# Levels of the block inverses: one group of eight steps in place of two groups of four

## The reference

```python
a_mat = eye + jnp.where(pos[:, None] > pos[None, :], beta[..., :, None] * decay * kk, 0.0)
gamma = jnp.exp(G)
rhs = jnp.concatenate([beta[..., None] * v, (beta * gamma)[..., None] * k], axis=-1)
sol = lax.linalg.triangular_solve(a_mat, rhs, left_side=True, lower=True, unit_diagonal=True)
v_t, w = sol[..., :dv], sol[..., dv:]
...
def step(h, xc):
    qg_c, pqk_c, vt_c, w_c, kd_c, gl_c = xc
    u = vt_c - jnp.einsum('bhck,bhkv->bhcv', w_c, h)
    o = jnp.einsum('bhck,bhkv->bhcv', qg_c, h) + jnp.einsum('bhcm,bhmv->bhcv', pqk_c, u)
    h = h * gl_c[..., None, None] + jnp.einsum('bhck,bhcv->bhkv', kd_c, u)
    return h, o
```

## Time and profile before

| | us |
|---|---|
| median of 3 runs | 3616.95 (3615.12 to 3622.28) |
| the profiled execution | 3621.84 |
| its span, first to last instruction | 3619.7 |
| PE busy | 3285.3 (91%) |
| DVE busy | 1534.0 (42%) |
| ACT busy | 1114.4 (31%) |
| mean granted TensorE clock | 0.941 of 2.4 GHz |

### The profile page before, as it was taken

One profiled execution on the slowest core, in us unless ns is written; L12 is line 12 of the kernel. 1 busy time (PEld: TensorE's weight loads), 2 busy tenths in 40 slices (PEclk: granted clock), 3 DMA queues, 4 the chain that ended last, 5 costly groups with the idle time before them and its releaser, 6 DMA issues. The chain is left out here.

```text
span 3619.7 us, 55834 instructions
## 1 busy us (share of the span) xinstructions
PE 3285.3 (91%) x23074; PEld 2753.0 (76%) x23074; DVE 1534.0 (42%) x2177; ACT 1114.4 (31%) x1426; POOL 71.3 (2%) x64
## 2 busy tenths in 40 slices
PE   4699999999999999999599967777778899999997
PEld 0477777777777888887388956666667899999997
DVE  0432313323233234233622456666634655555554
ACT  2221222212222222222522434333324544444443
POOL 0000000000000000000000001101100000000000
PEclk8799999999999999999799978888879899999998
DMA  9464464654645322233033600000033455555552
GB/s 374 174 234 169 179 243 163 229 188 170 241 169 209 105 93 93 93 104 128 24 93 118 184 15 2 2 2 2 2 118 127 140 185 183 177 184 184 180 181 82
DMA packets 313074, 501.24 MB, mean 138 GB/s; under 512 B 7932, under 2 KB 248068, under 8 KB 293124
## 3 DMA queue, kind: packets, MB, share of 16 engines
q1 hardware_dynamic: 311552, 495.15, 40.1%
q0 software_dynamic: 576, 4.19, 0.3%
q10 hardware_dynamic: 836, 0.33, 0.0%
HBM read 497.55 MB, written 2.10 MB: 138 GB/s over the span
## 5 line engine op out<-in xcount | busy, mean ns | idle before, releaser
L1555 PE MATMUL ps<-xn,parts 128*128 128x256 f32 (+1 forms) x11184 | 1908.9, 332 | 75.1 <-DVE xn L1266 50.6
L1555 PEld LDWEIGHTS ps<-xn,parts 128*128 128x128 f32 x11184 | 1687.1, 191 | 315.9 <-issue 92.9
L1132 DVE TENSOR_TENSOR parts<-raw,parts 128x1024 fp32r<-128x1024 f32 x642 | 766.0, 1223 | 1188.1 <-ACT parts L639 1180.4
L639 ACT ACTIVATE parts<-raw 128x1024 fp32r<-128x1024 f32 x638 | 660.7, 1055 | 1416.7 <-PE ps L1555 876.5
L1555 PE MATMUL ps<-h_parts,parts 128*128 128x512 f32 (+1 forms) x4224 | 739.1, 337 | 0.0
L1555 PEld LDWEIGHTS ps<-h_parts,parts 128*128 128x128 f32 x4224 | 649.6, 190 | 87.9 <-DVE h_f L1148 5.9
L1164 DVE TENSOR_TENSOR acc<-acc,ps 128x512 f32<-128x512 f32 (+1 forms) x352 | 193.0, 554 | 302.9 <-PE ps L1555 302.8
L1555 PE MATMUL ps<-raw,cpad 128*32 128x512 f32 x1152 | 157.4, 661 | 28.5 <-DMA raw<-in_w_mod 26.2
L1555 PEld LDWEIGHTS ps<-raw,cpad 128*32 128x32 f32 x1152 | 30.1, 114 | 121.9 <-DMA raw<-in_w_mod 61.6
L649 ACT ACTIVATE h_parts<-h_f 128x1024 fp32r<-128x1024 f32 (+1 forms) x44 | 37.2, 845 | 258.1 <-DVE h_f L1148 258.1
L1311 PE MATMUL ps<-g_T,g_C 64*64 64x64 f32 x1280 | 60.4, 246 | 56.8 <-DVE g_T L948 43.0
(11 more groups left out here) (195 smaller groups left out, 1506.0 us busy)
## 6 DMA issues: line engine op xcount, KB each, us to landing
raw<-in_w_mod SPq DMA_DIRECT2D x144, 1024.0 KB, 7.8
raw<-in_w_gate SPq DMA_DIRECT2D x88, 1024.0 KB, 5.1
raw<-in_w_up SPq DMA_DIRECT2D x88, 1024.0 KB, 5.1
raw<-in_w_down SPq DMA_DIRECT2D x88, 1024.0 KB, 5.1
raw<-in_w_in SPq DMA_DIRECT2D x41, 1024.0 KB, 5.3
raw<-in_w_out SPq DMA_DIRECT2D x16, 1024.0 KB, 5.5
x_in<-in_ctx SPq DMA_DIRECT2D x2, 1024.0 KB, 6.7
x_in<-in_x SPq DMA_DIRECT2D x2, 1024.0 KB, 12.0
```

The lines of the kernel that those rows point to most:

```text
L639: nc.scalar.activation(parts[:, unit % PART_SLOTS, 0, :], raw[:, slot, b * UNIT:(b + 1) * UNIT], ACT.Copy).then_inc(hi_ready, 1)
L1132: nc.vector.tensor_tensor(parts[:, pslot, 1, :], raw[:, slot, b * UNIT:(b + 1) * UNIT], parts[:, pslot, 0, :].bitcast(F32), ALU.subtract)\
L1555: return nc.tensor.matmul(o, lhsT, rhs, start=start, stop=stop)
```

## The change

The two groups become one of eight chunks. `y_level`, `x_level`, `y_out` and `level` lose their argument g and are called where g is 0; the places of group 1 stay empty. PSUM banks 0, 2 and 4 are used with all their 512 columns, and banks 1, 3 and 5 no more by these parts. The counts of the semaphores are halved, and the arithmetic is the same.

```diff
-            def y_out(a, lv, g):
+            def y_out(a, lv):
-                a.wait("y_mm", 2 * lv + g + 1)
+                a.wait("y_mm", lv + 1)
                 if lv:
-                    a.wait("x_mm", 2 * (lv - 1) + g + 1)
-                nc.scalar.activation(flat(grp(g_Y, g)), pair_cols(0, g), ACT.Copy).then_inc(hs["y_ok"], 1)
+                    a.wait("x_mm", lv)
+                nc.scalar.activation(flat(g_Y[:]), ps[:, 0, :], ACT.Copy).then_inc(hs["y_ok"], 1)
...
-            def level(a, lv, g):
+            def level(a, lv):
                 if lv < 4:
-                    a.wait("xt_mm", 2 * lv + g + 1)
-                    a.wait("t_ok", solved(lv, g))
-                    nc.vector.tensor_tensor(flat(grp(g_T, g)), flat(grp(g_T, g)), pair_cols(2, g),
-                                            ALU.subtract).then_inc(hs["t_ok"], 1)
-                a.wait("x_mm", 2 * lv + g + 1)
-                a.wait("s_ok", solved(lv, g))
-                nc.vector.tensor_tensor(flat(grp(g_S, g)), flat(grp(g_S, g)), pair_cols(4, g),
-                                        ALU.subtract).then_inc(hs["s_ok"], 1)
+                    a.wait("xt_mm", lv + 1)
+                    a.wait("t_ok", solved(lv))
+                    nc.vector.tensor_tensor(flat(g_T[:]), flat(g_T[:]), ps[:, 2, :], ALU.subtract)\
+                        .then_inc(hs["t_ok"], 1)
+                a.wait("x_mm", lv + 1)
+                a.wait("s_ok", solved(lv))
+                nc.vector.tensor_tensor(flat(g_S[:]), flat(g_S[:]), ps[:, 4, :], ALU.subtract)\
+                    .then_inc(hs["s_ok"], 1)
...
-                        if a:
-                            level(a, lv, g)
+                        if a and g == 0:
+                            level(a, lv)
...
-            def y_level(a, lv, g):
-                a.wait("t_ok", solved(lv, g))
+            def y_level(a, lv):
+                a.wait("t_ok", solved(lv))
...
-                for s in range(4 * g, 4 * g + 4):
-                    last = pair_mm(g, CHUNK * (s % 4), g_C[:, lv, s, :], g_T[:, s, :])
+                for s in range(STEPS):
+                    last = pair_mm(0, CHUNK * s, g_C[:, lv, s, :], g_T[:, s, :])
                 inc(last, "y_mm")
...
-            def x_level(a, lv, g):
-                a.wait("y_ok", 2 * lv + g + 1)
-                a.wait("s_ok", solved(lv, g))
+            def x_level(a, lv):
+                a.wait("y_ok", lv + 1)
+                a.wait("s_ok", solved(lv))
...
                 if lv < 4:
-                    for s in range(4 * g, 4 * g + 4):
-                        last = pair_mm(2 + g, CHUNK * (s % 4), g_S[:, s, :], g_Y[:, s, :])
+                    for s in range(STEPS):
+                        last = pair_mm(2, CHUNK * s, g_S[:, s, :], g_Y[:, s, :])
                     inc(last, "xt_mm")
-                for s in range(4 * g, 4 * g + 4):
-                    last = pair_mm(4 + g, CHUNK * (s % 4), g_Y[:, s, :], g_S[:, s, :])
+                for s in range(STEPS):
+                    last = pair_mm(4, CHUNK * s, g_Y[:, s, :], g_S[:, s, :])
                 inc(last, "x_mm")
...
                     for g in range(2):
-                        if a:
-                            y_level(a, lv, g)
+                        if a and g == 0:
+                            y_level(a, lv)
```

More of the change, by code:

```diff
@@ L257, in every, with solved @@
             return m.unsqueeze(1).to_broadcast([P, STEPS, m.shape[1]])
[L259 to L265, removed]
+        def solved(lv):
+            return lv + 1
         ps = es.enter_context(nc.psum_tensor("ps", [P, 8, 512], F32))
@@ L308, in build_layer @@
             "vb_ok": 2, "e_mm": 2, "e_exp": 2, "kk_mm": 1, "qk_mm": 1, "n_half": 1, "n_ok": 1, "p_half": 1,
-            "p_ok": 1, "nT_mm": 1, "nT_ok": 1, "ts_half": 2, "t_ok": 9, "s_ok": 11, "c_mask": 5, "y_mm": 10,
-            "y_ok": 10, "xt_mm": 8, "x_mm": 10, "w_mm": 1, "vt_mm": 2, "w_ok": 2, "vt_ok": 2,
+            "p_ok": 1, "nT_mm": 1, "nT_ok": 1, "ts_half": 2, "t_ok": 5, "s_ok": 6, "c_mask": 5, "y_mm": 5,
+            "y_ok": 5, "xt_mm": 4, "x_mm": 5, "w_mm": 1, "vt_mm": 2, "w_ok": 2, "vt_ok": 2,
             "f_stage": 1, "f_a": 1, "f_mid_ok": 1, "f_b": 1, "f_v": 1, "f_hi": 1, "f_lo": 1,
@@ L595, in step @@
                     for g in range(2):
-                        if a:
-                            y_out(a, lv, g)
+                        if a and g == 0:
+                            y_out(a, lv)
                         if b and lv < 2:
@@ L1402, in transposed @@
                 inc(last, "nT_mm")
-            def y_level(a, lv, g):
-                a.wait("t_ok", solved(lv, g))
+            def y_level(a, lv):
+                a.wait("t_ok", solved(lv))
                 a.wait("c_mask", lv + 1)
                 if lv:
-                    a.wait("y_ok", 2 * (lv - 1) + g + 1)
+                    a.wait("y_ok", lv)
                 else:
@@ L1411, in y_level @@
                     a.wait("f_v")
-                for s in range(4 * g, 4 * g + 4):
-                    last = pair_mm(g, CHUNK * (s % 4), g_C[:, lv, s, :], g_T[:, s, :])
+                for s in range(STEPS):
+                    last = pair_mm(0, CHUNK * s, g_C[:, lv, s, :], g_T[:, s, :])
                 inc(last, "y_mm")
-            def x_level(a, lv, g):
-                a.wait("y_ok", 2 * lv + g + 1)
-                a.wait("s_ok", solved(lv, g))
+            def x_level(a, lv):
+                a.wait("y_ok", lv + 1)
+                a.wait("s_ok", solved(lv))
                 if lv == 0:
-                    a.wait("vb_ok", g + 1)
+                    a.wait("vb_ok")
                     a.wait("p_half")
                 if lv < 4:
-                    for s in range(4 * g, 4 * g + 4):
-                        last = pair_mm(2 + g, CHUNK * (s % 4), g_S[:, s, :], g_Y[:, s, :])
+                    for s in range(STEPS):
+                        last = pair_mm(2, CHUNK * s, g_S[:, s, :], g_Y[:, s, :])
                     inc(last, "xt_mm")
-                for s in range(4 * g, 4 * g + 4):
-                    last = pair_mm(4 + g, CHUNK * (s % 4), g_Y[:, s, :], g_S[:, s, :])
+                for s in range(STEPS):
+                    last = pair_mm(4, CHUNK * s, g_Y[:, s, :], g_S[:, s, :])
                 inc(last, "x_mm")
@@ L1539, in step @@
                             written_u(b, STEPS - 1)
-                        if a:
-                            x_level(a, lv, g)
+                        if a and g == 0:
+                            x_level(a, lv)
                         if b and lv < 2:
```

## The result

Over 20 runs each, the kernel before takes 3617.93 us (3615.04 to 3622.41) and the changed one 3625.59 us (3623.83 to 3630.35): 7.7 us more, ratio 1.002, interval [1.0013, 1.0027]. That lies in the range of the prediction (3611 to 3634), 4.6 us above its forecast and just over the 0.2% that it takes for the limit of a measurement: slower, to which it gave a chance of 0.26, against 0.66 for no difference that can be told.

The account below looks back on a forecast made before the run. The mixer was taken as a relay with no engine full, bound by late hand-overs. Terms 1.4 + 1.8 + 0.9 = +4.1 us took the profiled 3621.84 to 3625.9; with the median 4.9 lower, the forecast was 3621.0, range 3611 to 3634.

Parts of the forecast that it names:

- The prices of the instructions: Mixer: one 512-column DVE subtraction takes 0.684 us, one 512-column ACT copy 0.597 us, both taken from similar instructions.
- B: Rival, faster: DVE's time decides and hand-overs cost nothing; 2.8 us saved over nine levels, 3614 us; chance 0.11.
- The hand-overs in heads 1 to 6: Middle heads: wider copies and subtractions hand over later, +0.3 us a head (ends +0.1 and +0.6), +1.8 for six.
- Head 0: First head, no scan beside it: later hand-overs in levels 1 to 4, +1.4 us (ends +0.6 and +1.6).
- The +0.6 behind it: First head, level 4 after y: x starts 0.35 us later and the last subtraction adds 0.26.
- Head 7: Last head, no convolutions: level 3 +0.6 us, last subtraction +0.26; sum +0.9 (ends +0.6 and +1.3).
- After the change it stands behind both: Middle heads, level 0: u_buf comes behind both halves' subtractions, so the product with kd_b starts 0.5 us later.
- That wait becomes 2.1 us or so: Middle heads, level 1: u_buf and its product stay 0.5 us late, so PE's wait of 1.67 us grows.
- Rival A: Slower: clock falls once more behind level 1's wait, at best 6.6 us low, 3.3 lost a head; 3636 us; chance 0.19.
- Rival C: Faster: clock holds through the solve; heads 0 and 7, 3614.5 us, chance 0.12; all eight, 3595 us, chance 0.04.
- D: Rival, slower: level 1's +0.5 us does not come back in level 2, six times 0.5 more; 3624 us; chance 0.12.

Follow-up runs that it names:

- the repair: Changed kernel with DVE's u_buf subtraction of step 6 moved behind the first three of level 0's six convolutions; 3616.88 us, ratio 0.9996.
- fill_level1: Changed kernel with two useless 128x256 matmuls on PE ahead of step 6's product, in level 1 of heads 1 to 6; 3618.62 us, ratio 1.000.

## Why the prediction was right in its range, and where it was wrong

**The prices of the instructions** (0.684, 0.597): right within 0.003 us. **B** is refuted: DVE's and ACT's busy time fell as computed and nothing came of it, and with DVE's subtractions alone merged the ratio was 1.0012. The rule of the Trainium skill that was weighed there (TensorEngine Tiling (Array Packing), PSUM Bottleneck) holds for the busy time, 0.685 us for one against 0.84 for two, but here the reading of PSUM was not the limit.

**The hand-overs in heads 1 to 6** (+0.3 each, ends 0.1 and 0.6): right. In the heads that no low stretch disturbs, 2, 4 and 6, the levels take 36.0 us against a mean of 35.6 for the six heads before, +0.4; with all waits filled, heads 1 to 5, which are disturbed in both kernels (4) or in neither, differ by +0.37, +0.38, +0.22, +0.40 and -0.13.

**Head 0** (+1.4): right. Its y of level 4 comes 0.83 later after its first y, as forecast (0.8). The +0.6 behind it doesn't show against the trace of the kernel before, whose last level and solve of head 0 run at the low clock. It shows against the trace of the kernel before with two useless matmuls in level 1, where head 0's code is unchanged and its solve runs at the full clock: levels 22.27 and 23.68 us, periods 48.23 and 49.63, +1.4 both times. The stretch from kbg on, in the kernel before and in that run:

```profile
2181.80:2189.40 7.60, 7.28 (x64) 6.76 (x64) 1.19 (x5) 2.02 (x5) 0.00 (x0) 0.50 0.01 2
...
2183.00:2190.60 7.60, 6.81 (x125) 6.46 (x126) 2.23 (x8) 4.33 (x8) 0.00 (x0) 1.00 0.01 2
```

**Head 7** (+0.9): from its y of level 1 to kbg it is +0.96 in both pairs, plain and with filled waits (18.97 to 19.93), but not by the steps of the sum: level 1 +0.4, level 2 -0.2, level 3 +0.8 (forecast 0.6), level 4 nothing (forecast 0.26). Level 0, for which the sum had no term, adds 0.5, so it is +1.4 from the first y, just beyond the end of 1.3.

So the sum that made the forecast, +4.1, measured 1.4 + 2.2 + 1.4 = +5.0 in the plain traces (0.36 a middle head by the periods of heads 2, 4 and 6), and +3.5 where the waits are filled. Two of its steps were wrong:

- *Level 0, "After the change it stands behind both", +0.5*: the product was later by 0.45 (9.58 against 9.13 us after the first y), but not for that reason. The releaser is ACT's qh, which waits for a product that PE issues behind the whole of x. The run with u_buf ahead of g_S shows it. The size was right by accident.
- *Level 1, where u_buf and the product "keep the +0.5", so "That wait becomes 2.1 us or so"*: from the product of step 5 to that of step 6 it is 4.12 us, and the wait is 1.74 us. Before it was 4.12 with a wait of 1.50 in the five other heads, and 4.29 with 1.67 in head 3, my pattern. So the product doesn't come later after the one before it: PE runs out of work 0.24 us earlier (2.38 us after that product in place of 2.62), and the order on PE alone does that, since the run with only this order has the same 4.12 and 1.74 in five heads.

**Rival A** has the mechanism and the place: the clock falls once more, after level 1's wait. It was given a chance of 0.19 and the time 3636, with "at best the shortest low stretch seen", 6.6 us. That term was mis-sized: the stretch was 3.4 us, in three heads of six. Its cost is 1.14 us in the levels (37.14 against 36.00), and 1.4 more in the same head's solve, whose low stretch is 17.0 us in place of 10.2: 2.5 us a head (periods of 67.84 against 65.31), 7.6 in three. The argument against A, "the scan's products lie in this stretch", did not hold; they did not keep the clock up.

Why every second head? The wait is 1.74 us in all six. In heads 1, 3 and 5 it begins 3.59, 3.53 and 3.53 us after the end of level 0's low stretch, in heads 2, 4 and 6 3.35, 3.32 and 3.32 (the ends of the stretches taken from the trace's record of the clock, finer than the 0.2 us of the table). The two other kernels with this wait (one of 1.91 among them) agree: 3.42 to 3.74 in the five disturbed heads, 3.15 to 3.34 in the seven others. Other waits show that 3.4 us is no fixed bound. Waits of 1.50 us began up to 3.43 after it in the kernel before, 3.80 with DVE alone merged and 4.09 with ACT alone merged, and the clock held. One of 1.67 held at 3.17 (head 3 before); behind one of 1.66 at 3.50 it fell (head 3 with ACT alone merged). Waits of 1.82 held at 2.89 to 3.20 and fell at 3.35, and one of 2.00 fell at 3.29, both earlier than my expectation of that run allowed (3.44); 2.46 fell from 3.07 on. So length and place of the wait both seem to count. Each extra stretch lengthens its head and so shifts the next one, which would explain why the two kinds alternate. That the shift decides was read from the traces; no run shifted a head on purpose.

**Rival C** (0.12 for two heads, 3.3 us each) came in for head 7: its solve is at the full clock and 10.2 us less are at the low one, and 4.9 us come back (4.4 in the filled pair). For head 0 the solve is at the full clock too, worth 4.2 us from first y to first y (48.2 against 52.4). The change isn't needed for that: head 0's code of the kernel before did it in two of five traces (that with three repeats of u_buf and that with two useless matmuls). The changed kernel did it in all four traces without filled waits around level 4; whether the change makes it surer isn't shown. This is most likely also why the runs of the kernel before lie in two groups: its own trace, with head 0's solve at the low clock, took 3621.84 us, and that with the two useless matmuls, with the full one, 3617.76.

**D** is refuted. From y to y, head 4 after the change against head 3 before, level 0 is 0.66 longer (10.48 to 9.82), level 1 0.13 shorter (head 3 is the odd one: against the other heads it is 0.04 longer), level 2 0.21 shorter (5.62 to 5.83, forecast 0.3), level 3 0.20 shorter (forecast: within 0.1), level 4 up to kbg 0.22 longer (forecast 0.48): +0.34 in all.

Together, in the terms of the traces, with head 0's solve at the full clock on both sides: hand-overs 1.4 + 2.2 + 1.4 = +5.0, clock in heads 1, 3 and 5 +7.6, head 7's solve -4.9: +7.7, as the medians have it. That it fits to the tenth is luck: in the trace of the kernel before with two useless matmuls heads 1 and 2 are another 1.5 us shorter, and the first y moves by 3 us from trace to trace. Of the 4.6 us by which the forecast was too low, 1.0 is the median that it started from (3616.95, now 3617.93), 0.9 the hand-overs, and 2.7 what A took less what C gave, two terms that the sum had at nothing. The range held in part by luck: A's 7.6 us and C's 4.9 came together, which the prediction didn't foresee. What stays open is why the last solve keeps the clock. It does so in the changed kernel, and its like from kbg to the end is 986.7 us with DVE alone merged and 987.9 with PE's order alone, against 990.1 before and 990.2 with ACT alone merged; no run shows which wait decides it.

## What to carry to other kernels

Where PE's clock moves, judge a reordering first by what it does to PE's idle stretches, and only then by the work that it saves: 0.24 us more of a wait cost more here (7.6 us) than all the hand-overs together (5.0), and 0.34 us more of it 13 to 16 us. Look through all repetitions of a wait, not through one head, before taking its length as the pattern. When an edit costs more than its terms, fill the suspected wait with matmuls that nothing reads: if the time comes back while the late product stays late, it was the clock, and an order that brings the late producer forward is the clean repair.

## What the runs showed of the hardware

- The clock's answer to a wait is not in proportion. In the kernel before, a level 1 wait of 1.50 to 1.67 us brought no low stretch, one of 1.82 to 2.00 us two stretches of 13.6 us in six heads (11 us lost), 2.46 us six stretches of 3.4 to 7.0.
- At 1.2 GHz the same product lasts nearly twice as long (1.92 against 1.10 us for 32 instructions), and in the changed kernel the stretch reaches beyond its cause: 17.0 us in the solve of every head that had an extra one, 10.2 in those that had none. This is no rule: with PE's order alone head 4 had an extra one and 10.2 in its solve, and with DVE alone merged heads 3 and 5 had 17.0 without one.
- With PE work without use in four waits of a head, either kernel is 33 to 35 us (0.9 to 1%) under the kernel before, more than any order of the useful work tried here gave.
- What one place of the program gains, a longer low stretch later can take back: 1.5 us of levels in each head, period unchanged at 64.8 us (the repair against fill_level1).
